# The overflow branch ahead of the last down products, and the last half summed in PSUM by quarters

## The chip, the cores and the metric

One core of one Trainium2 chip runs the program. The time is microseconds (us) of device time for one execution; the kernel before was timed three times, and one further execution was profiled. Every number stored or multiplied is 32-bit float.

## The reference, cut to what matters

A sequence of 256 tokens of 1024 features passes two mixing layers, and then two transformer layers that each end in a mixture of experts. What the change touches is the end of each of those two:

```
y   = hierarchical_moe(h, ...)      # 32 experts: (silu(x @ w_gate[e]) * (x @ w_up[e])) @ w_down[e],
                                    # for the tokens that chose e, each row times its gate,
                                    # summed back over the tokens
x   = layer_norm(ALPHA * x + (1 + g2) * y, ln_g[i, 1], ln_b[i, 1])
```

`w_gate` and `w_up` are 1024 x 512 per expert, `w_down` 512 x 1024: 6 MB an expert, 192 MB a layer, all streamed from HBM.

## The kernel before, in words

The block is written as one instruction list per engine (TensorE, VectorE, ScalarE, GpSimd, SyncE), with semaphores between them. A helper class `Engine` counts what an engine has waited for (`past`) and signalled (`n`). A PSUM bank is taken with `begin(b, name)` (TensorE waits until its last content is drained), signalled with `filled(name)`, and given back by its reader with `drained(name)`.

Experts run in `NQ` = 8 quads of four (`experts(i)`, layer `i` = 0 or 1), with up to `CAP` = 32 tokens of each expert in fixed places. Of a quad `q` TensorE does: the gate and up products of its experts `j` = 0..3 (L920, matmuls of 128 columns, four column groups of 32 at once), a transpose of each hidden tile (`hidden(j)`, L449), a transpose of the gates (`gsT`), the down products of the four experts side by side on the partitions (banks 5 and 6 hold columns 0..511 and 512..1023), and `combine(n)` (L983), which multiplies half `n` with the transposed gates `GST` and so adds it back to the tokens of both token tiles `t`. VectorE multiplies each down half by the gate row `G2` into `YS` (L1062), then adds each combined bank to the running sum `ACC`, which is the array `X` (L1062).

The last quad differs. Its down weights come as three rows of four (`("row", f)`, 2 MB each) and two ends (`("end", n)`, 1 MB each), so that little work is left when the last piece lands. TensorE spreads the two rows of the closing layer norm over the partitions (`norm_row`, L888, banks 1 and 4), does the rows (`down_rows`, L965), the second norm row, the end of half 0 (`down_end`, L973), `combine(0)`, the end of half 1, and `combine(1)`. VectorE follows: multiply, two adds, two `bn_stats` (L1440) for each half, then `last_norm`: two aggregations (L1447), with GpSimd's reciprocal root in parallel, and two passes of `scalar_tensor_tensor` over each token tile's 1024 columns (L1070).

If any expert has over 32 tokens, a slow path `overflow(i)` handles the rest. Whether it runs is read at run time from `cnt`, set early in the layer. TensorE asks after its last `combine` (L1053 and L1054), VectorE after the last quad's hidden tiles (L1822 and L1823), ScalarE and SyncE after their work of the layer. With the inputs here the slow path isn't taken, so each engine jumps over the whole of `overflow`, which is unrolled over 32 experts.

SyncE issues all weight loads, in an order and into slots that a planner fixes beforehand (`plan`); after the last load of layer 0 it asks the same question and then goes on with the loads of the next layer's attention. In layer 0 TensorE's next work after the question is `grouped()`: two gate rows of the attention (L493), which need nothing of the expert stage but free banks, then transposes of `X` (L449).

Of the kernel before, what the change touches and what calls it, by code (L numbers as in the profile page):

```python
# [14 lines left out]
NT = 2  # L15
# [24 lines left out]
NE = 32  # L40
# [88 lines left out]
def program(nc, A, out):  # L129
    with ExitStack() as ctx:  # L130
# [240 lines left out]
        def rows_of_four(i, f):  # L371
            return piece(("dn", i, NQ - 1, "row", f), 4, 1024)
# [61 lines left out]
        def _(eng):  # L434
            pe = Engine(eng, sem("pe"))

            def begin(b, *name):
                if n_results[b]:
                    pe.wait_ge(sem(f"drained{b}"), n_results[b])
                n_results[b] += 1  # L440
                RESULT[name] = b, n_results[b]
                return banks[b]
# [447 lines left out]
            def experts(i):  # L890
# [12 lines left out]
                for q in range(NQ):  # L903
# [39 lines left out]
                    def down(n):  # L943
# [10 lines left out]
                                DONE[name] = filled("dn", i, q, n)  # L954
                        end(ins, "dn", i, q, n)

                    def down_rows():
                        o = [begin(5 + n, "dn", i, q, n) for n in range(2)]
                        for j in range(4):
                            pe.wait_ge(*drained("aT", i, q, j))  # L960
                        for f in range(3):
                            pe.wait_ge(*loaded("dn", i, q, "row", f))
                            for n in range(2):
                                for j in range(4):
                                    ins = eng.matmul(o[n][32 * j:32 * j + 32, :], AT[u][:, j, 32 * f:32 * f + 32],  # L965
                                                     rows_of_four(i, f)[:, j, 512 * n:512 * n + 512], start=f == 0, stop=False)
                            DONE["dn", i, q, "row", f] = pe.step(ins)
                        return o

                    def down_end(o, n):  # L970
                        pe.wait_ge(*loaded("dn", i, q, "end", n))
                        for j in range(4):
                            ins = eng.matmul(o[n][32 * j:32 * j + 32, :], AT[u][:, j, 96:128], ends_of_four(i, n)[:, j, :],  # L973
                                             start=False, stop=True)
                        end(ins, "dn", i, q, n)
                        DONE["dn", i, q, "end", n] = filled("dn", i, q, n)

                    def combine(n):
                        for t in range(NT):
# [3 lines left out]
                            end(eng.matmul(o[:, :], GST[u][:, 128 * t:128 * t + 128], YS[:, 512 * n:512 * n + 512],  # L983
                                           start=True, stop=True), "cb", i, q, n, t)

                    if q == NQ - 1:
                        norm_row(2 * i + 1, 0, LN_OUT[0])
                        o = down_rows()
                        norm_row(2 * i + 1, 1, LN_OUT[1])
                        down_end(o, 0)  # L990
                        combine(0)
                        down_end(o, 1)
                    else:
                        down(0)
                        down(1)
                        combine(0)
                    combine(1)


            def overflow(i):  # L1000
# [45 lines left out]
            for i in range(DEPTH):  # L1046
                if i:
                    grouped()
                else:
                    neighbourhood()  # L1050
                router(i)
                experts(i)
                pe.wait_ge(sem("cnt"), i + 1)  # L1053
                with eng.If(eng.value_load(cnt[0:1, NE:NE + 1]) > CAP):  # L1054
                    overflow(i)

        @block.vector
        def _(eng):
# [662 lines left out]
            def experts(i, chosen):  # L1721
# [17 lines left out]
                for q in range(NQ):  # L1739
# [72 lines left out]
                        combine(1)  # L1812
                        continue

                    def end():
                        for n in range(2):
                            down(n)
                            combine(n)


                    v.wait_ge(sem("cnt"), i + 1)
                    kept = v.n, dict(v.past), v.last  # L1822
                    with eng.If(eng.value_load(cnt[0:1, NE:NE + 1]) > CAP):  # L1823
                        end()
                        overflow(i)
                    v.n, v.past, v.last = kept
                    with eng.Else():
                        end()

            def overflow(i):  # L1830
                o_pe, o_v, o_s = sem(f"o_pe{i}"), sem(f"o_v{i}"), sem(f"o_s{i}")
# [34 lines left out]
                eng.wait_ge(o_pe, O_PE_END)  # L1866


            def last_norm(i):
                for t in range(NT):  # L1870
                    deviation(t)
                for n in range(2):
                    for h in range(2):
                        v.wait_ge(*drained("row", 2 * i + 1, n, h))
                for t in range(NT):
                    v.step(stt(X[:, t, :], X[:, t, :], bn_a[:, t, 0:1], LN_OUT[0], ALU.subtract, ALU.mult))
                v.chain()
                for t in range(NT):
                    v.wait_ge(sem("lrs"), n_dev[0] - 1 + t)
                    ins = stt(X[:, t, :], X[:, t, :], st2[:, t:t + 1], LN_OUT[1], ALU.mult, ALU.add)  # L1880
                    if i + 1 < DEPTH:
                        v.tell(ins, sem("xn"), 3 + t)
                    else:
                        v.tell(ins, sem("xl"), t + 1)
# [3 lines left out]
            for i in range(DEPTH):  # L1888
                if i:
                    grouped()  # L1890
                else:
                    neighbourhood()
                experts(i, router(i))
                last_norm(i)

        @block.scalar
        def _(eng):
# [701 lines left out]
```

## Time and profile before

| | |
|---|---|
| median of 3 runs | 1532.74 us (1531.36 to 1538.42) |
| the profiled execution, its own time | 1536.27 us |
| its span, first to last instruction | 1534.5 us |
| mean granted TensorE clock | 0.951 |
| TensorE busy | 1376.1 us, 90% |
| VectorE busy | 547.8 us, 36% |
| DMA queue of the weights | 519.40 MB |

The span is what the trace covers. A page of the profile names the chain of work that ended last; a timeline gives each merged group of instructions with its start, its length, and in brackets how long its engine had been idle before it and what ended that. PE is TensorE, PEld its weight loads, DVE VectorE, ACT ScalarE, POOL GpSimd, SP SyncE. A 32-bit matmul of the code appears as two MATMUL records.

### The profile page before, as it was taken

What the parts mean: (1) busy time and instruction counts of PE and PEld (TensorE: products, weight loads), DVE (VectorE), ACT (ScalarE), POOL (GpSimd) and SP (SyncE); (2) the same over time, 40 slices, a digit from 0 to 9 for tenths busy, and PEclk for the clock granted to TensorE, in tenths of its full rate; (3) what the DMA queues carried; (4) which work ended last, traced back from release to release, by engine and by line L of the source; (5) the groups of instructions that cost most, each with busy time, mean ns of one, the idle gap of its engine ahead of it and who ended that gap; (6) DMA issues with size and microseconds to landing.
All of it is one profiled execution on the core that took longest, in us unless ns stands there. A gap on an engine that the chain in (4) does not pass through costs nothing.

```text
span 1534.5 us, 28540 instructions
## 1 busy us (share of the span) xinstructions
PE 1376.1 (90%) x12866; PEld 874.1 (57%) x12866; DVE 547.8 (36%) x1251; ACT 218.1 (14%) x578; POOL 85.4 (6%) x91
## 2 busy tenths in 40 slices
PE   7999999999999998879879788878999798798796
PEld 4886488578886555436435443467665363354451
DVE  3596659665843221111111105583211111111113
ACT  3230123022332000000000001442100000000000
POOL 3100111000003000000000001100200000000000
PEclk9999999999999999889889999989999898898997
DMA  9657945778869999999999997237999999999994
GB/s 345 225 195 261 333 171 202 285 267 306 311 270 353 421 427 426 428 426 425 428 426 426 427 399 278 106 121 316 423 410 426 426 426 428 427 426 426 428 420 178
DMA packets 94552, 531.23 MB, mean 346 GB/s; under 512 B 5184, under 2 KB 7424, under 8 KB 70608
## 3 DMA queue, kind: packets, MB, share of 16 engines
q1 hardware_dynamic: 91264, 519.40, 83.8%
q0 software_dynamic: 3152, 9.86, 1.9%
q8 instruction: 105, 1.72, 0.4%
q14 instruction: 31, 0.25, 0.0%
HBM read 528.19 MB, written 1.05 MB: 345 GB/s over the span
## 4 chain that ended last, share of the span: by engine, by line
PE 61%; DMA 29%; DVE 7%; ACT 1%; issue 1%; DVEq 0%; SPq 0%; ACTq 0%
PE bk L453 26%; PE bk L920 16%; DMA AR<-in_moe_w_down 14%; DMA ring<-in_moe_w_down 14%; PE bk L952 8%; PE bk L983 4%; DVE mpart L1070 3%; PE bk L449 2%; PE bk L672 2%; ACT AR L1901 1%; PE bk L687 1%; DVE AR L1062 1%; PE bk L643 1%; DMA ring<-in_w_in 1%; DVE sm L1073 1%
## 5 line engine op out<-in xcount | busy, mean ns | idle before, releaser
L920 PE MATMUL bk<-ring,AR 128*32 128x128 f32 x4480 | 267.5, 409 | 3.1 <-DMA ring<-in_moe_w_up 3.1
L920 PE MATMUL bk<-AR 128*32 128x128 f32 x3712 | 223.0, 409 | 4.8 <-DMA AR<-in_moe_w_up 4.0
L1062 DVE TENSOR_TENSOR AR<-bk,AR 128x128 f32<-128x128 f32 (+2 forms) x106 | 41.3, 390 | 516.9 <-ACT AR L1901 450.4
L920 PEld LDWEIGHTS bk<-ring,AR 128*32 128x32 f32 x4480 | 175.4, 127 | 85.6 <-DMA ring<-in_moe_w_up 5.6
L453 PE MATMUL bk<-ring,AR 128*128 128x256 f32 (+2 forms) x736 | 214.3, 449 | 5.7 <-ACT AR L1901 2.6
L1901 ACT ACTIVATE AR<-bk 128x512 f32<-128x512 f32 (+4 forms) x182 | 75.3, 436 | 931.9 <-PE bk L920 755.9
L920 PEld LDWEIGHTS bk<-AR 128*32 128x32 f32 x3712 | 144.8, 127 | 75.3 <-DMA AR<-in_moe_w_up 6.2
L453 PEld LDWEIGHTS bk<-ring,AR 128*128 128x128 f32 x736 | 141.3, 195 | 71.4 <-issue 54.4
L952 PE MATMUL bk<-ring,AR 128*32 128x512 f32 x544 | 137.5, 704 | 43.1 <-DMA ring<-in_moe_w_down 43.1
L453 PE MATMUL bk<-AR,ring 128*128 128x256 f32 (+1 forms) x832 | 170.6, 364 | 1.6 <-DVE diag L1062 1.6
L453 PEld LDWEIGHTS bk<-AR,ring 128*128 128x128 f32 x832 | 147.4, 190 | 21.4 <-issue 3.5
L952 PE MATMUL bk<-AR 128*32 128x512 f32 x352 | 130.8, 714 | 27.4 <-DMA AR<-in_moe_w_down 27.4
L1070 DVE SCALAR_TENSOR_TENSOR mpart<-ring,ccol,mpart 128x512 f32<-128x512 f32 x168 | 130.3, 776 | 6.0
L1062 DVE TENSOR_TENSOR AR<-bk,mpart 128x512 f32<-128x512 f32 x32 | 22.1, 691 | 218.8 <-PE bk L952 191.4
L952 PEld LDWEIGHTS bk<-ring,AR 128*32 128x32 f32 x544 | 31.0, 126 | 103.3 <-DMA ring<-in_moe_w_down 57.8
L449 PE MATMUL bk<-cst,AR 128*128 128x128 f32 (+1 forms) x356 | 63.9, 292 | 22.6 <-DVE AR L1746 12.0
L449 PEld LDWEIGHTS bk<-cst,AR 128*128 128x128 f32 (+1 forms) x356 | 41.3, 142 | 57.3 <-issue 26.2
L453 PE MATMUL bk<-AR 128*128 128x128 f32 (+1 forms) x536 | 71.2, 292 | 0.6 <-DVE AR L1062 0.5
L952 PEld LDWEIGHTS bk<-AR 128*32 128x32 f32 x352 | 28.4, 127 | 72.5 <-DMA AR<-in_moe_w_down 38.5
L453 PEld LDWEIGHTS bk<-AR 128*128 128x128 f32 x536 | 65.9, 199 | 4.7 <-issue 2.6
L983 PE MATMUL bk<-AR 128*128 128x512 f32 x128 | 61.1, 619 | 5.0 <-DVE AR L1062 5.0
L643 PE MATMUL bk<-ring,AR 128*128 128x512 f32 x128 | 55.5, 594 | 0.0
(161 smaller groups left out, 892.0 us busy)
## 6 DMA issues: line engine op xcount, KB each, us to landing
ring<-in_moe_w_gate SPq DMA_DIRECT2D x36, 2048.0 KB, 30.0
ring<-in_moe_w_up SPq DMA_DIRECT2D x34, 2048.0 KB, 26.8
AR<-in_moe_w_up SPq DMA_DIRECT2D x30, 2048.0 KB, 29.6
ring<-in_moe_w_down SPq DMA_DIRECT2D x30, 2048.0 KB, 34.2
AR<-in_moe_w_gate SPq DMA_DIRECT2D x28, 2048.0 KB, 27.3
AR<-in_moe_w_down SPq DMA_DIRECT2D x26, 2048.0 KB, 34.0
ring<-in_ada_w SPq DMA_DIRECT2D x24, 2048.0 KB, 10.7
ring<-in_w_in SPq DMA_DIRECT2D x12, 2048.0 KB, 14.4
```

The costliest lines, as they stand in the source:

```text
L449: return eng.transpose(o, a, ident[0:k, 0:k])
L453: ins = eng.matmul(o, l, r, start=i == 0, stop=i == len(pairs) - 1)
L643: ins = eng.matmul(o[:, :], BIG[:, x, OUTS[m] + 128 * t:OUTS[m] + 128 * t + 128], w[:, 2 * m + x, :], start=k + x == 0, stop=k + x == 4)
L672: ins = eng.matmul(o[b][:, a * nk:(a + 1) * nk], g["q"][h][:, t * 128:(t + 1) * 128], g["k"][h][:, 0:nk], start=True, stop=True)
L687: ins = eng.matmul(o[64 * b:64 * b + 64, 128 * x:128 * x + 128], g["v"][2 * x + b][kt], ET[j % 2][:, (2 * b + x) * nkt + kt, :], start=kt ...
L920: ins = eng.matmul(o[32 * f:32 * f + 32, 128 * m:128 * m + 128], XG[u][:, c, 32 * j:32 * j + 32], w[:, c, f::4], start=c == 0, stop=c == N ...
L952: ins = eng.matmul(o[32 * j:32 * j + 32, :], AT[u][:, j, 32 * f:32 * f + 32], w, start=f == 0, stop=f == 3)
L983: end(eng.matmul(o[:, :], GST[u][:, 128 * t:128 * t + 128], YS[:, 512 * n:512 * n + 512], start=True, stop=True), "cb", i, q, n, t)
L1062: return eng.tensor_tensor(o, a, b, op)
L1070: return eng.scalar_tensor_tensor(out=o, in0=a, scalar=s, in1=b, op0=op0, op1=op1)
L1073: return eng.tensor_reduce(o, a, AX, op)
L1901: return eng.activation(o, a, f, **kw)
```

## The change

Both ends of the last quad are rewritten.

On TensorE the question whether there is overflow is asked before the last quad's down products, and everything after it stands in both arms (`ending()`; `overflow(i)` follows in one of them). Inside `ending()`, two products with the identity first put the running sum of half 1 (`ACC[:, t, 512:1024]`) into banks 2 and 3 and leave them open. Half 1 of the down products is split into two quarters of 256 columns, in banks 6 and 0; `combine(1)` becomes `end_sums`, which adds each quarter's product with the gates onto the open banks, quarter by quarter.

On VectorE the multiply of half 1 comes in two quarters, and the adds of half 1 are gone: `bn_stats` reads the banks, and `last_norm`, now in both arms, reads half 1 of its first pass from the banks too. In the overflow arm the banks are copied to `ACC` first.

```diff
--- before.py
+++ after.py
@@ -954,26 +954,48 @@
                                 DONE[name] = filled("dn", i, q, n)
                         end(ins, "dn", i, q, n)
 
+                    halves = ((0, (("dn", i, q, 0), 5, 0, 512)), (1, (("quarter", i), 6, 512, 256)), (1, (("dn", i, q, 1), 0, 768, 256)))
+
                     def down_rows():
-                        o = [begin(5 + n, "dn", i, q, n) for n in range(2)]
+                        o = [begin(b, *name)[:, 0:c] for n, (name, b, c0, c) in halves]
                         for j in range(4):
                             pe.wait_ge(*drained("aT", i, q, j))
                         for f in range(3):
                             pe.wait_ge(*loaded("dn", i, q, "row", f))
-                            for n in range(2):
+                            for k, (n, (name, b, c0, c)) in enumerate(halves):
                                 for j in range(4):
-                                    ins = eng.matmul(o[n][32 * j:32 * j + 32, :], AT[u][:, j, 32 * f:32 * f + 32],
-                                                     rows_of_four(i, f)[:, j, 512 * n:512 * n + 512], start=f == 0, stop=False)
+                                    ins = eng.matmul(o[k][32 * j:32 * j + 32, :], AT[u][:, j, 32 * f:32 * f + 32],
+                                                     rows_of_four(i, f)[:, j, c0:c0 + c], start=f == 0, stop=False)
                             DONE["dn", i, q, "row", f] = pe.step(ins)
                         return o
 
                     def down_end(o, n):
                         pe.wait_ge(*loaded("dn", i, q, "end", n))
-                        for j in range(4):
-                            ins = eng.matmul(o[n][32 * j:32 * j + 32, :], AT[u][:, j, 96:128], ends_of_four(i, n)[:, j, :],
-                                             start=False, stop=True)
-                        end(ins, "dn", i, q, n)
+                        for k, (m, (name, b, c0, c)) in enumerate(halves):
+                            if m == n:
+                                for j in range(4):
+                                    ins = eng.matmul(o[k][32 * j:32 * j + 32, :], AT[u][:, j, 96:128],
+                                                     ends_of_four(i, n)[:, j, c0 - 512 * n:c0 - 512 * n + c], start=False, stop=True)
+                                end(ins, *name)
                         DONE["dn", i, q, "end", n] = filled("dn", i, q, n)
+
+                    def begin_sums():
+                        o = []
+                        for t in range(NT):
+                            o.append(begin((2, 3)[t], "cb", i, q, 1, t))
+                            pe.wait_ge(*drained("cb", i, q - 1, 1, t))
+                            eng.matmul(o[t][:, :], ident, ACC[:, t, 512:1024], start=True, stop=False)
+                        return o
+
+                    def end_sums(o):
+                        pe.wait_ge(*drained("gsT", i, q))
+                        for c0 in (0, 256):
+                            pe.wait_ge(*(drained("dn", i, q, 1) if c0 else drained("quarter", i)))
+                            for t in range(NT):
+                                ins = eng.matmul(o[t][:, c0:c0 + 256], GST[u][:, 128 * t:128 * t + 128],
+                                                 YS[:, 512 + c0:768 + c0], start=False, stop=c0 > 0)
+                                if c0:
+                                    end(ins, "cb", i, q, 1, t)
 
                     def combine(n):
                         for t in range(NT):
@@ -983,18 +1005,31 @@
                             end(eng.matmul(o[:, :], GST[u][:, 128 * t:128 * t + 128], YS[:, 512 * n:512 * n + 512],
                                            start=True, stop=True), "cb", i, q, n, t)
 
-                    if q == NQ - 1:
+                    if q < NQ - 1:
+                        down(0)
+                        down(1)
+                        combine(0)
+                        combine(1)
+                        continue
+
+                    def ending():
+                        sums = begin_sums()
                         norm_row(2 * i + 1, 0, LN_OUT[0])
                         o = down_rows()
                         norm_row(2 * i + 1, 1, LN_OUT[1])
                         down_end(o, 0)
                         combine(0)
                         down_end(o, 1)
-                    else:
-                        down(0)
-                        down(1)
-                        combine(0)
-                    combine(1)
+                        end_sums(sums)
+
+                    pe.wait_ge(sem("cnt"), i + 1)
+                    kept = pe.n, dict(pe.past), pe.last, list(n_results)
+                    with eng.If(eng.value_load(cnt[0:1, NE:NE + 1]) > CAP):
+                        ending()
+                        overflow(i)
+                    pe.n, pe.past, pe.last, n_results[:] = kept
+                    with eng.Else():
+                        ending()
 
 
             def overflow(i):
@@ -1050,9 +1085,6 @@
                     neighbourhood()
                 router(i)
                 experts(i)
-                pe.wait_ge(sem("cnt"), i + 1)
-                with eng.If(eng.value_load(cnt[0:1, NE:NE + 1]) > CAP):
-                    overflow(i)
 
         @block.vector
         def _(eng):
@@ -1812,20 +1844,35 @@
                         combine(1)
                         continue
 
-                    def end():
-                        for n in range(2):
-                            down(n)
-                            combine(n)
+                    def end(stored):
+                        down(0)
+                        combine(0)
+                        v.wait_ge(*filled("cb", i, q - 1, 1, 1))
+                        for k, name in enumerate((("quarter", i), ("dn", i, q, 1))):
+                            v.wait_ge(*filled(*name))
+                            free(tt(YS[:, 512 + 256 * k:768 + 256 * k], bank(*name)[:, 0:256], G2[1][:, 256 * k:256 * k + 256],
+                                    ALU.mult), *name)
+                        for t in range(NT):
+                            o = bank("cb", i, q, 1, t)[:, :]
+                            v.wait_ge(*filled("cb", i, q, 1, t))
+                            if stored:
+                                free(eng.tensor_copy(ACC[:, t, 512:1024], o), "cb", i, q, 1, t)
+                                v.chain()
+                                v.step(stats(t, 1, ACC))
+                            else:
+                                v.step(eng.bn_stats(bn_s[:, t, 1, :], o))
 
 
                     v.wait_ge(sem("cnt"), i + 1)
-                    kept = v.n, dict(v.past), v.last
+                    kept = v.n, dict(v.past), v.last, n_dev[0]
                     with eng.If(eng.value_load(cnt[0:1, NE:NE + 1]) > CAP):
-                        end()
+                        end(True)
                         overflow(i)
-                    v.n, v.past, v.last = kept
+                        last_norm(i, True)
+                    v.n, v.past, v.last, n_dev[0] = kept
                     with eng.Else():
-                        end()
+                        end(False)
+                        last_norm(i, False)
 
             def overflow(i):
                 o_pe, o_v, o_s = sem(f"o_pe{i}"), sem(f"o_v{i}"), sem(f"o_s{i}")
@@ -1866,14 +1913,19 @@
                 eng.wait_ge(o_pe, O_PE_END)
 
 
-            def last_norm(i):
+            def last_norm(i, stored):
                 for t in range(NT):
                     deviation(t)
                 for n in range(2):
                     for h in range(2):
                         v.wait_ge(*drained("row", 2 * i + 1, n, h))
                 for t in range(NT):
-                    v.step(stt(X[:, t, :], X[:, t, :], bn_a[:, t, 0:1], LN_OUT[0], ALU.subtract, ALU.mult))
+                    if stored:
+                        v.step(stt(X[:, t, :], X[:, t, :], bn_a[:, t, 0:1], LN_OUT[0], ALU.subtract, ALU.mult))
+                        continue
+                    v.step(stt(X[:, t, 0:512], X[:, t, 0:512], bn_a[:, t, 0:1], LN_OUT[0][:, 0:512], ALU.subtract, ALU.mult))
+                    free(stt(X[:, t, 512:1024], bank("cb", i, NQ - 1, 1, t)[:, :], bn_a[:, t, 0:1], LN_OUT[0][:, 512:1024],
+                             ALU.subtract, ALU.mult), "cb", i, NQ - 1, 1, t)
                 v.chain()
                 for t in range(NT):
                     v.wait_ge(sem("lrs"), n_dev[0] - 1 + t)
@@ -1891,7 +1943,6 @@
                 else:
                     neighbourhood()
                 experts(i, router(i))
-                last_norm(i)
 
         @block.scalar
         def _(eng):
```

## Rows read from the trace of the kernel before

**Rows 1.** the page: GB/s in 40 slices; last chain by engine
```profile
GB/s 345 225 195 261 333 171 202 285 267 306 311 270 353 421 427 426 428 426 425 428 426 426 427 399 278 106 121 316 423 410 426 426 426 428 427 426 426 428 420 178
...
PE 61%; DMA 29%; DVE 7%; ACT 1%; issue 1%; DVEq 0%; SPq 0%; ACTq 0%
```

**Rows 2.** the chain that ended last: start, us, what
```profile
926.99 4.92 issue
```

**Rows 3.** timeline, PE, layer 0: start, us, what, count [idle before]
```profile
905.35 0.33 PE L449 MATMUL bk<-cst,AR 128*128 128x128 f32 x1 [0.52 <-DVE AR L1778]
...
905.61 1.98 PE L888 MATMUL bk<-AR,ones 1*128 1x512 f32 x4
...
907.52 3.62 PE L965 MATMUL bk<-ring,AR 128*32 128x512 f32 x16
...
914.75 1.92 PE L965 MATMUL bk<-AR 128*32 128x512 f32 x16 [1.89 <-DMA AR<-in_moe_w_down]
...
920.48 1.96 PE L983 MATMUL bk<-AR 128*128 128x512 f32 x4 [0.91 <-DVE AR L1062]
...
922.37 1.06 PE L973 MATMUL bk<-ring,AR 128*32 128x512 f32 x8
...
925.01 1.99 PE L983 MATMUL bk<-AR 128*128 128x512 f32 x4 [1.57 <-DVE AR L1062]
...
931.91 2.08 PE L493 MATMUL bk<-diag,ones 64*128 64x512 f32 x4 [4.92 <-issue]
...
933.92 3.68 PE L449 MATMUL bk<-cst,X 128*128 128x128 f32 x16
```

**Rows 4.** timeline, SyncE at the same end: the issue of DMAs
```profile
900.62 0.51 SPq L2495 DMA_DIRECT2D ring<-in_moe_w_down  x1
...
906.91 15.00 SPq L2404 DMA_DIRECT2D ring<-in_gqa_w_qkv  x3
```

**Rows 5.** timeline, layer 1's last quad, PE
```profile
1500.43 0.33 PE L449 MATMUL bk<-cst,AR 128*128 128x128 f32 x1 [0.52 <-DVE AR L1778]
...
1509.96 1.92 PE L965 MATMUL bk<-AR 128*32 128x512 f32 x16 [0.38 <-DMA AR<-in_moe_w_down]
...
1511.81 1.98 PE L888 MATMUL bk<-AR,ones 1*128 1x512 f32 x4
...
1515.69 3.38 PE L983 MATMUL bk<-AR 128*128 128x512 f32 x4 [0.90 <-DVE AR L1062]
```

**Rows 6.** timeline, PE: 64 products of 128 columns in four groups
```profile
887.14 7.57 PE L920 MATMUL bk<-AR 128*32 128x128 f32 x128
```

**Rows 7.** windows: length, busy of five engines, granted clock, DMA, GB/s
```profile
907.00:908.00 1.00, 1.00 (x6) 0.19 (x8) 0.00 (x0) 0.74 (x2) 0.00 (x0) 0.79 1.03 395
...
911.00:912.00 1.00, 1.00 (x16) 0.35 (x12) 0.00 (x0) 0.00 (x0) 0.00 (x0) 1.00 0.85 332
...
931.00:932.00 1.00, 0.09 (x2) 0.12 (x2) 1.00 (x1) 0.00 (x0) 0.40 (x1) 0.74 1.05 391
...
1501.00:1502.00 1.00, 1.00 (x3) 0.40 (x2) 0.09 (x1) 0.00 (x0) 0.00 (x0) 0.75 1.02 403
...
1508.00:1509.00 1.00, 1.00 (x16) 0.21 (x8) 0.00 (x0) 0.00 (x0) 0.00 (x0) 0.84 0.58 229
```

**Rows 8.** timeline, layer 0's end, DVE
```profile
923.08 1.28 DVE L1440 BATCH_NORM_STATS2 st<-X 128x6 f32<-128x512 f32 x2
...
924.28 0.68 DVE L1062 TENSOR_TENSOR AR<-bk,mpart 128x512 f32<-128x512 f32 x1
...
927.63 1.28 DVE L1440 BATCH_NORM_STATS2 st<-X 128x6 f32<-128x512 f32 x2
...
929.71 5.00 DVE L1070 SCALAR_TENSOR_TENSOR X<-X,st,AR 128x1024 f32<-128x1024 f32 x4
```

**Rows 9.** groups by form, DVE: what xcount | busy us, mean ns | idle
```profile
L1062 DVE TENSOR_TENSOR AR<-bk,AR 128x256 f32<-128x256 f32 x24 | 10.2, 423 | 39.1 <-PE bk L453 38.2 <-PE bk L687 0.7
...
L1070 DVE SCALAR_TENSOR_TENSOR X<-X,bk 128x512 f32<-128x512 f32 x8 | 5.5, 688 | 1.7 <-PE bk L983 1.7
```

## The prediction

> **What bounds the kernel now.** I read the page first: bytes a second and the last chain by engine. While experts stream, the core moves about 426 GB/s slice after slice, and the chain goes through TensorE and DMA with little else [rows 1]. So time lost or won at the end of a layer, where the next layer or the output waits for it, is not paid back by a faster stream: the loads of the second layer's experts wait for slots that its attention frees. Second, the chain in order of time: right after layer 0's last combine it has a piece called issue, 4.92 us in which TensorE waits for nothing that the profile knows [rows 2]. Third, the timelines of both layer ends on TensorE, SyncE and VectorE. The reader is to see three things there. The last hidden transpose ends at 905.68 (layer 0) and 1500.76 (layer 1). The third row of down weights is then waited for, but barely: 1.89 us in layer 0, 0.38 us in layer 1, so the last matmuls on it end at 916.67 and 1511.88 [rows 3, 5]. Behind that TensorE and VectorE alternate until the norm.
>
> **The moved branch.** The 4.92 us lie exactly where the overflow question stands now: between the last record of `combine` (ends 926.99) and the gate rows of the next attention (931.91). Those gate rows need a diagonal that VectorE wrote long before and banks that were drained before 926.99. I take the time as the price of load, compare and jump on TensorE. A second row bounds it: SyncE asks the same question after its last issue (ends 901.13) and issues the next load at 906.91, into a slot whose last reader, the up products of expert 29, was long done; that is 5.8 us [rows 4]. SyncE asks it while the stream is full, at nearly the place to which TensorE's question moves. So TensorE's costs 4.9 us from the end of the last transpose, or 5.8 us from its start (the sequencer can run ahead of the array): it restarts at 910.6 to 911.15, I take 910.9; in layer 1 at 1505.7 to 1506.2, I take 1506.0. Queued behind it on TensorE is everything that is left of the layer, and VectorE and ScalarE wait for that; SyncE and GpSimd are not moved past.
>
> The Trainium skill speaks on both sides here. "Runtime: NRT & Kernel Launch", section Instruction fetch mechanics, says that a taken jump to code outside the small window of fetched instructions has to wait for a DMA fetch; the jump here passes the unrolled slow path, and the rows agree in sign. "Advanced Engine Details and Errata", section Control Flow Timing, gives about 108 ns for a compare and branch; at that price the branch would vanish from the sum (second rival).
>
> **What TensorE does before the third row is done.** In the changed kernel, from its restart:
> - two identity products of 512 columns, four records like `combine(0)`'s, whose successor starts 1.89 us later (920.48 to 922.37) [rows 3]: 1.9 us, new;
> - the first norm row: 905.61 to 907.52, 1.9 us, as before;
> - three rows of down weights. Sixteen records of 512 columns take 1.85 us at full clock (1509.96 to 1511.81) [rows 5]. Now eight of 512 and sixteen of 256: the first eight cost 0.93 us; for the others the floor is the issue, 7.57 us / 128 = 0.059 us a record [rows 6], 0.94 us. That is 1.87 us, I take 1.9 with some slack: 5.7 us for three.
> That is 9.5 us at full clock. The weights are there by then: the third row landed at 914.7 and 1509.9.
>
> The clock is the unsure term. In layer 0 it fell to half (1.2 GHz) within 907 to 908 and was back at 911; in layer 1 it fell within 1501 to 1502 and was back only in 1508 to 1509; after the 4.9 us of idling at the branch it fell again, at 931 to 932 [rows 7]. A mean of 0.79 in a window between full and half says that it fell at 907.6, and 0.75 and 0.84 that it was low from 1501.5 to 1508.3. Both stretches (3.4 and 6.8 us) lay in the shadow of the third row's landing. Now TensorE idles first and then has work it can't hide, so half of the half-clock time is lost: 1.7 to 3.4 us if the whole stretch falls on work, 0.9 us if part of it falls into the idling. I take 2.2 us in each layer. Sum: layer 0 910.9 + 9.5 + 2.2 = 922.6, 5.9 us later than 916.67; layer 1 1506.0 + 9.5 + 2.2 = 1517.7, 5.8 us later than 1511.88. The cover that was used up is 1.9 and 0.4 us of waiting and the slow clock's shadow; all else is on the path.
>
> **What the new end saves.** Half 1's multiply can't start before VectorE has done half 0's statistics (923.08 to 924.36), as now at 924.28 [rows 8]. A multiply of 256 columns takes 0.42 us [rows 9], pitch about 0.34: both quarters are ready at 924.70 and 925.04. TensorE adds the first quarter for two tiles (half of 1.89: 0.9 us, from 924.75), then the second, tile 0 ready about 926.15, tile 1 about 926.6. `bn_stats` on the banks then runs to about 927.5. Now it ends at 928.91 [rows 8]. A saving of 1.4 us. Reading statistics from PSUM has no row; on VectorE a 512-wide pass from a bank takes 688 ns [rows 9], and `bn_stats` from `X` takes 1.28 us for two, so I bound the difference by 0.1 us either way. The closing pass of two 1024-wide instructions (pitch 1.25 us) [rows 8] becomes four of 512 (pitch about 0.6 to 0.69, by the 688 ns row): from 0 to 0.3 us more, I take 0.1. Net 1.3 us a layer. The half-1 end itself (sixteen records of 256 for eight of 512) costs 0 to 0.1 us, hidden by the statistics that the multiply waits for.
>
> Layer 0 also gets back part of the old branch: the gate rows at 931.91 to 933.99 held back the transposes of `X`, ready at about 933.5 (929.71 [rows 8] and three passes of 1.25 us) and started at 933.92 [rows 3], and the ScalarE copies behind them. Taken with the earlier `X` I count 1.8 us there in place of 1.3, with 0 to 0.3 us more possible. In layer 1 the branch lay beside the norm and gives nothing back. Layer 1's `combine(0)` ran at half clock, 3.38 us, where layer 0's took 1.96 [rows 3, 5]; in the change it may or may not, so half of 1.4, 0.7 us, is counted as a gain.
>
> **Sum.** Layer 0: +5.9 - 1.8 = +4.1. Layer 1: +5.8 - 1.3 - 0.7 = +3.8. Together +7.9 us. The profiled execution's own time is 1536.27 us (span 1534.5 plus 1.8 around it), which gives 1544.2; it lies 3.5 us above the median but inside the runs. The terms are differences, so I put them on the median, 1532.74, and round up: 1541 us. Lowest terms (restart at 910.6 and 1505.7, clock loss 0.9, tail 1.4 and 1.9, clock gain 1.4): +3.8, 1536.5. Highest (911.15 and 1506.2, clock loss 3.4, tail 0.9 and 1.4, no clock gain, 0.1 more in the rows): +12.5, 1545.2.
>
> **Rivals.**
> *More half clock.* For: with TensorE later, pieces like `combine(0)` with 0.9 us gaps on both sides may fall into half clock in both layers, 1.4 us each, as layer 1's did [rows 5]; the low stretch can last 6.8 us [rows 7]. Against: the same gaps in layer 0 passed at full clock. Time: the sum's upper half plus 1.4 to 2.8, 1545 to 1549, about 1546.
>
> *The branch is cheap where it goes, so not slower.* The mechanism: the jump's price at 926.99 is something of that place (a fetch into the next layer's code), and TensorE restarts at once behind the last transpose. Then only the identity products delay it. Layer 0's third row could begin at 912.86 (914.75 - 1.89), now 914.85: 0.1 us late. Layer 1's at 1509.58 plus 1.9 to 3.4 us (full or half clock), 1511.5 to 1513.0 for 1509.96: about 2.4 us late. With the gains of 1.8 and 2.0 this is +0.1 - 1.8 + 2.4 - 2.0 = -1.3: 1531.5, between 1529.5 and 1533. It decides from a branch of under 1 us. For: VectorE asks at the same point and the trace shows no price for it, though its wait for the down products would hide one. Against: SyncE's 5.8 us. The 108 ns that the Trainium skill gives would lead here too.
>
> *The new end fails to shorten.* If reading PSUM or the open banks made VectorE wait, the tail would save 0 in place of 1.3 us a layer: +10.5, 1543. Against: the 512-wide pass with a bank as operand takes no more than its share of the 1024-wide one from `X` (688 ns of 1.25 us, with a fixed part in both) [rows 8, 9].
>
> **How the numbers follow.** Forecast 0.65, more half clock 0.15, cheap branch 0.13, no shorter end 0.07. The measurement tells 0.5%, 7.7 us: 1525.1 and 1540.4. The forecast's own range, 1536 to 1546, is split by 1540.4 nearly in the middle; with 0.15 and 0.07 all above it, slower by over 0.5% gets 0.52, no difference 0.44, faster 0.04 (even the cheap branch gives only 1 to 3 us). Range 1532 to 1547: it leaves out the lower half of the cheap branch and the end of more half clock.
>
> **What would show it.** Right: in the changed trace TensorE idles some 5 us with "issue" between the last hidden transpose and the first identity product in both layers; the third down row starts without a wait for DMA, about 5 to 6 us later than now; the gate rows L493 follow the last sums with under 1 us of idling; statistics end about 1.4 us sooner after the second end's products. Wrong: idling of under 1 us in front of the identity products (second rival), a third row that still waits for its DMA, or a granted clock that stays full.

## The result, and the profile after

The changed kernel took 1554.41 us (median of 4, 1552.67 to 1558.16) against 1535.58 us of the kernel before on the same chip (median of 4, 1531.36 to 1538.48): ratio 1.0125, 95% interval 1.0102 to 1.0148, or +18.8 us at the medians. The direction was forecast, the size was not: +7.9 us was said, and 1547 was the end of the range.

The page of the changed kernel, its span and the last chain by engine:

```profile
span 1551.5 us, 28698 instructions
...
PE 65%; DMA 24%; DVE 8%; issue 2%; ACT 1%; DVEq 0%; SPq 0%; ACTq 0%
```

Against [rows 1] the chain has more TensorE and less DMA, but that tells little: a run below that is no slower than the kernel before (e8) has 63% and 26%, with layer 0's third row still waiting 1.92 us for its DMA. The timelines decide.

The timeline of TensorE at layer 0's last quad, changed kernel, beside [rows 3]:

```profile
900.86 0.33 PE L449 MATMUL bk<-cst,AR 128*128 128x128 f32 x1 [0.52 <-DVE AR L1810]
...
907.56 3.78 PE L987 MATMUL bk<-X,cst 128*128 128x512 f32 x4 [6.37 <-issue]
...
911.27 3.78 PE L888 MATMUL bk<-AR,ones 1*128 1x512 f32 x4
...
918.39 3.89 PE L967 MATMUL bk<-AR 128*32 128x512 f32 x48
...
922.21 1.98 PE L888 MATMUL bk<-AR,ones 1*128 1x512 f32 x4
...
926.09 3.48 PE L1005 MATMUL bk<-AR 128*128 128x512 f32 x4 [0.90 <-DVE AR L1094]
...
929.50 1.07 PE L977 MATMUL bk<-ring,AR 128*32 128x256 f32 x16
...
933.79 1.13 PE L493 MATMUL bk<-diag,ones 64*128 64x512 f32 x4
...
939.68 3.48 PE L449 MATMUL bk<-cst,X 128*128 128x128 f32 x16 [4.75 <-DVE X L1102]
```

Identity products, norm row and down rows now stand in a line without a wait for DMA. (A group x48 on L967 holds two rows of down weights, 24 records each.) I count from the start of the last transpose, since single executions reach it some us apart (905.35 before, 900.86 here), to the last record on the third row: 11.3 us before (905.35 to 916.67), 21.4 us now (900.86 to 922.28). Layer 1, beside [rows 5]:

```profile
1508.38 0.33 PE L449 MATMUL bk<-cst,AR 128*128 128x128 f32 x1 [0.52 <-DVE AR L1810]
...
1514.88 3.78 PE L987 MATMUL bk<-X,cst 128*128 128x512 f32 x4 [6.17 <-issue]
...
1525.72 4.01 PE L967 MATMUL bk<-AR 128*32 128x512 f32 x48
...
1529.66 1.98 PE L888 MATMUL bk<-AR,ones 1*128 1x512 f32 x4
...
1533.54 3.54 PE L1005 MATMUL bk<-AR 128*128 128x512 f32 x4 [0.90 <-DVE AR L1094]
```

It was 11.45 us (1500.43 to 1511.88) and is 21.4 us (1508.38 to 1529.73). So each layer's third row is done 10 us later after the transpose, where 5.8 and 5.9 were forecast. The windows show why; the granted clock is the first number behind the five engines:

```profile
901.00:902.00 1.00, 0.19 (x1) 0.00 (x0) 0.29 (x1) 0.00 (x0) 0.00 (x0) 0.93 0.99 393
...
918.00:919.00 1.00, 1.00 (x12) 0.36 (x8) 0.00 (x0) 0.00 (x0) 0.00 (x0) 0.54 1.06 399
...
1509.00:1510.00 1.00, 0.00 (x0) 0.00 (x0) 0.04 (x1) 0.00 (x0) 0.00 (x0) 0.72 1.01 395
...
1526.00:1527.00 1.00, 1.00 (x12) 0.15 (x8) 0.00 (x0) 0.00 (x0) 0.00 (x0) 0.75 0.00 0
```

A mean between 0.5 and 1 tells how much of that microsecond was at half clock (1.2 GHz). The clock falls 0.7 us into the idling, at 901.9 and 1509.4, is at 0.50 in every window between, and comes back only at 918.9 and 1526.5: 17.1 us each, of which 11.4 and 11.6 us are work (907.56 to 918.9, 1514.88 to 1526.5).

VectorE at layer 0's end, beside [rows 8]:

```profile
930.21 1.28 DVE L1472 BATCH_NORM_STATS2 st<-X 128x6 f32<-128x512 f32 x2
...
933.47 1.29 DVE L1863 BATCH_NORM_STATS2 st<-bk 128x6 f32<-128x512 f32 x2 [1.32 <-PE bk L995]
...
935.57 0.75 DVE L1102 SCALAR_TENSOR_TENSOR X<-X,st,AR 128x512 f32<-128x512 f32 x1
...
938.34 2.48 DVE L1102 SCALAR_TENSOR_TENSOR X<-X,st,AR 128x1024 f32<-128x1024 f32 x2
```

From the start of the last end products to the last statistics: 922.37 to 928.91 before, 6.5 us; 929.50 to 934.76 now, 5.3 us; layer 1 has the same two numbers. The new end saves its 1.3 us.

### The profile page after: what moved, and what is told of

Its sections match the earlier page's. It is cut to its first block, busy times and chain, and to the rows that moved or that the text cites. A ratio compares the mean times of both kernels' runs of the same rounds, so it can differ in the third digit from the quotient of the medians.

```text
span 1551.5 us, 28698 instructions
## 1 busy us (share of the span) xinstructions
PE 1385.7 (89%) x12946; PEld 883.4 (57%) x12946; DVE 545.7 (35%) x1253; ACT 217.8 (14%) x578; POOL 84.4 (5%) x91
## 4 chain that ended last, share of the span: by engine, by line
PE 65%; DMA 24%; DVE 8%; issue 2%; ACT 1%; DVEq 0%; SPq 0%; ACTq 0%
PE bk L453 26%; PE bk L920 19%; DMA ring<-in_moe_w_down 14%; DMA AR<-in_moe_w_down 9%; PE bk L952 8%; PE bk L1005 4%; DVE mpart L1102 3%; PE bk L449 2%; PE bk L672 1%; ACT AR L1952 1%; DVE AR L1094 1%; PE bk L687 1%; PE bk L967 1%; PE bk L643 1%; PE bk L888 1%
## 5 line engine op out<-in xcount | busy, mean ns | idle before, releaser
L453 PE MATMUL bk<-ring,AR 128*128 128x256 f32 (+2 forms) x736 | 210.4, 443 | 5.5 <-ACT AR L1952 2.7
L453 PEld LDWEIGHTS bk<-AR,ring 128*128 128x128 f32 x832 | 147.4, 190 | 21.4 <-issue 3.5
L1094 DVE TENSOR_TENSOR AR<-bk,mpart 128x512 f32<-128x512 f32 (+1 forms) x34 | 22.2, 659 | 239.8 <-PE bk L952 192.4
## 6 DMA issues: line engine op xcount, KB each, us to landing
ring<-in_ada_w SPq DMA_DIRECT2D x24, 2048.0 KB, 10.9
ring<-in_w_in SPq DMA_DIRECT2D x12, 2048.0 KB, 14.7
```

Of the source, the lines that this page charges most:

```text
L453: ins = eng.matmul(o, l, r, start=i == 0, stop=i == len(pairs) - 1)
L1094: return eng.tensor_tensor(o, a, b, op)
```

## The experiments

All ratios are to the kernel before on the same chip, whose medians were 1537.08 (e1 to e4), 1537.54 (e6 to e9) and 1535.59 us (e5, e10, e12). A signed time is the ratio less 1, times this median; the difference of the two medians can lie up to 3 us off it. The diffs are abridged. "Transpose to third row" is the interval of the section above: 11.3 and 11.45 us before, 21.4 and 21.4 in the changed kernel. Theory A: the question idles TensorE where it has no slack, and the idling drops the clock over the work behind it. Theory B: the identity products are what costs.

**e1, only the question moves.**

```diff
 # kernel before, TensorE, last quad
+def ending():                      # the old end, unchanged
+    norm_row(0); down_rows; norm_row(1); down_end(0); combine(0); down_end(1); combine(1)
+pe.wait_ge(sem("cnt"), i + 1)
+with eng.If(count > CAP):
+    ending()
+    overflow(i)
+with eng.Else():
+    ending()
```

> Only the question moves: TensorE asks before the last quad's down products, with the old end in both arms; no identity products, no quarters. Theory A (the question idles TensorE for about 6.4 us and the clock is then at half over the work behind it): the third down row is done 6 to 7 us later after the last transpose than in the kernel before, in each layer, and combine(0) may fall into half clock too (1.5 us); layer 0 gets 1 to 2 us back from the old place. Sum +11 to +16 us. Theory B (the identity products in front of the rows are what costs, the question is largely hidden by the wait for the weights): +0 to +5 us.

1551.41 us, ratio 1.0102 (1.0084 to 1.0119), +15.7 us. TensorE, layer 0:

```profile
901.39 0.33 PE L449 MATMUL bk<-cst,AR 128*128 128x128 f32 x1 [0.52 <-DVE AR L1787]
...
908.07 3.78 PE L888 MATMUL bk<-AR,ones 1*128 1x512 f32 x4 [6.35 <-issue]
...
911.77 3.64 PE L965 MATMUL bk<-ring,AR 128*32 128x512 f32 x16
...
915.19 3.96 PE L965 MATMUL bk<-AR 128*32 128x512 f32 x32
```

The idle is 6.35 us, norm row and first down row run at half clock (3.7 and 3.4 us to the next group), and the third row is done 17.8 us (layer 1: 17.6 us) after the transpose: +6.3 a layer. The clock was at half for 13.7 us (902.2 to 915.9), the last 7.8 of them with work. `combine(0)` took 3.53 us in layer 0, 1.6 us more than in [rows 3]. Theory A holds; the question alone makes about four fifths of the loss (0.0102 of 0.0125).

**e2, only the new end.**

```diff
 # changed kernel, TensorE
-with eng.If(...): ending(); overflow(i)
-with eng.Else(): ending()
+ending()                           # question behind it, as before
```

> Only the new end: identity products, quarters, statistics and norm from the banks; TensorE asks after the end, as before. Theory A: no idle in front, so the identity products cost 1.9 us, in layer 0 under the wait for the third row, in layer 1 1.5 to 3.4 us on the path; the tails save 1.3 us each. Sum -1 to +2 us against the kernel before. Theory B: +10 us or more.

1534.92 us, ratio 0.9984 (0.9968 to 1.0000), -2.5 us: a little under the expected -1 to +2, and with an interval that ends at 1. Theory B falls. TensorE in layer 1, and then the old question's place in layer 0:

```profile
1501.58 0.33 PE L449 MATMUL bk<-cst,AR 128*128 128x128 f32 x1 [0.52 <-DVE AR L1806]
...
1501.75 1.88 PE L987 MATMUL bk<-X,cst 128*128 128x512 f32 x4
...
1510.23 1.93 PE L967 MATMUL bk<-AR 128*32 128x512 f32 x24 [1.11 <-DMA AR<-in_moe_w_down]
```

```profile
932.07 2.08 PE L493 MATMUL bk<-diag,ones 64*128 64x512 f32 x4 [5.28 <-issue]
```

The identity products start 0.17 us behind the transpose and run at full clock (1.88 us), and the third row still waits 1.11 us for its DMA: they cost nothing on the path. The question is back behind the end, 5.28 us. `combine(0)` is at half clock in both layers here too (3.53 and 3.65 us), with no question in front: so full or half clock there varies between runs with the question behind the end, and its 1.5 us can't be booked to the question alone.

**e3, the jump made short.**

```diff
 with eng.If(count > CAP):
     ending()
-    overflow(i)
```

> The changed kernel without the slow path in TensorE's overflow arm (it is left out there, so the arm is a few hundred instructions); load, compare and both arms stay. If the price of the question is the jump past the unrolled slow path (code has to be fetched): the idle in front of the identity products falls from 6.4 us to 1 to 2.5 us, and the time to about +5 to +9 us over the kernel before. If it is the load of the count and the compare: it stays near 6.4 us and +18 us.

1538.46 us, ratio 1.0019 (0.9995 to 1.0044), not told apart from the kernel before and under the +5 to +9 us that I expected. TensorE, layer 0:

```profile
901.98 0.33 PE L449 MATMUL bk<-cst,AR 128*128 128x128 f32 x1 [0.52 <-DVE AR L1809]
...
903.45 1.98 PE L987 MATMUL bk<-X,cst 128*128 128x512 f32 x4 [1.14 <-issue]
...
911.38 1.93 PE L967 MATMUL bk<-AR 128*32 128x512 f32 x24 [0.46 <-DMA AR<-in_moe_w_down]
```

The idle is 1.14 us here and 0.54 us in layer 1. From the start of the transpose to the first identity product it is 1.5 and 0.9 us, where the changed kernel has 6.7 and 6.5. So load, compare, two arms and a jump over a few hundred instructions are cheap; over 5 us come with the jump past the unrolled slow path. The clock stays full, the third row waits for its DMA again, and it is done 11.3 and 11.4 us after the transpose, as in the kernel before: nothing is left of the 10 us a layer.

The Trainium skill states in "Runtime: NRT & Kernel Launch", section Instruction fetch mechanics, that a taken jump out of the window of fetched instructions stalls until its target is fetched by DMA. These rows agree with it; they show the dependence on the distance, not the fetch itself. The Trainium skill's 108 ns for a compare and branch, in "Advanced Engine Details and Errata", section Control Flow Timing, are not what either question cost here (0.54 us of idle at the least).

**e4, the array kept busy over the question.**

```diff
+busy(8, 5)       # 8 identity products of 512 columns into bank 5, used by nobody
 pe.wait_ge(sem("cnt"), i + 1)
```

> The changed kernel with eight more identity products of 512 columns (16 records, 6.9 us at full clock) issued just before the question, into a free bank; their results are used by nobody. If TensorE's sequencer runs ahead of its array, the array works while the question is answered, the clock stays full, and the third row is done 4 to 5 us sooner in each layer than in the changed kernel: about +9 us over the kernel before. If the question waits for the array to drain: the idle of 6.4 us follows the products, and the time is +25 us or more (theory A holds on the idle but the clock can't be saved so).

1542.93 us, ratio 1.0040 (1.0022 to 1.0057), +6 us. TensorE, layer 0:

```profile
902.06 0.33 PE L449 MATMUL bk<-cst,AR 128*128 128x128 f32 x1 [0.52 <-DVE AR L1811]
...
902.23 7.03 PE L869 MATMUL bk<-cst 128*128 128x512 f32 x16
...
909.10 1.88 PE L987 MATMUL bk<-X,cst 128*128 128x512 f32 x4
...
914.56 3.63 PE L967 MATMUL bk<-AR 128*32 128x512 f32 x48
```

Sixteen records fill 902.23 to 909.26 and the real work follows with no gap: the sequencer answers the question while the array works. All is at full clock, 16.1 us from transpose to third row in both layers, 5.3 us less than in the changed kernel, though the real work begins 7.0 us behind the transpose and not 6.7. Up to the third row this run keeps the delay and takes away only the slow clock. From the first identity product to the third row it is 9.1 us here and 14.7 us in the changed kernel (907.56 to 922.28): 5.6 us a layer is the slow clock's price. The total is below the +9 us expected: twice 5.3 us at the third rows, and 1.5 us more because `combine(0)` took 1.95 us in layer 0, at full clock.

**e5, without the identity products.**

```diff
-eng.matmul(o[t][:, :], ident, ACC[:, t, 512:1024], start=True, stop=False)
 ...
-    start=False, stop=c0 > 0)
+    start=c0 == 0, stop=c0 > 0)
```

> The changed kernel without the two identity products: the running sum of half 1 is left out of the result, all else stays. If they cost what they take at half clock and nothing else: third row 3.7 us sooner after the last transpose in each layer, about -7 us against the changed kernel, +10 to +11 us against the kernel before. If the clock comes back by the clock time and not by the work done, the stretch at half clock shifts onto the down rows, and they save only about 2 us a layer: +14 us. The rival in which the identity products are the main cost: +2 us or less.

1549.11 us, ratio 1.0081 (1.0054 to 1.0109), +12.4 us; the result lacks the running sum of half 1. Transpose to third row 17.9 and 18.1 us, close to e1, and the clock at half for 13.7 us as there. In the changed kernel, behind the idling, the products cost about 3.4 us a layer, a little less than the 3.7 us that they take at half clock; in e2 they cost nothing.

**e6 and e8, the question where TensorE waits anyway.**

```diff
 # TensorE, experts(i): the body of the loop over quads becomes quad(q) -> front, back
+for q in range(6): front(q); back(q)
+front(6)
+with eng.If(count > CAP): back(6); front(7); back(7); overflow(i)
+with eng.Else():          back(6); front(7); back(7)
```

> The changed kernel with the question one quad earlier on TensorE, in front of the seventh quad's down products, everything behind it in both arms. There TensorE waits some 7 us for down weights in any case. Theory A (the price is idling and slow clock where TensorE has no slack): the 6.4 us lie inside that wait, the last quad runs as in e2, and layer 0 has no question behind its end: -2 to -4 us against the kernel before, 13 us or more faster than the changed kernel. Rival (the two arms or the jump cost wherever they stand): +6 us or more.

> The kernel before with its question moved in front of the seventh quad's down products, old end unchanged. Theory A: hidden by the wait for weights, and layer 0's end is rid of its 4.9 us idle, of which 0.5 to 1 us was on the path: -0.5 to -1.5 us against the kernel before. Rival as for e6: +6 us.

e6 (new end): 1534.09 us, ratio 0.9993 (0.9973 to 1.0012). e8 (old end): 1538.50 us, ratio 1.0014 (0.9999 to 1.0029). e6 in the seventh quad of layer 0, and its last quad:

```profile
842.25 3.74 PE L453 MATMUL bk<-AR 128*128 128x128 f32 x32
...
850.55 1.03 PE L953 MATMUL bk<-AR 128*32 128x512 f32 x1 [4.57 <-issue]
```

```profile
902.69 0.33 PE L449 MATMUL bk<-cst,AR 128*128 128x128 f32 x1 [0.52 <-DVE AR L1823]
...
911.86 1.93 PE L968 MATMUL bk<-AR 128*32 128x512 f32 x24 [1.63 <-DMA AR<-in_moe_w_down]
...
925.36 1.13 PE L493 MATMUL bk<-diag,ones 64*128 64x512 f32 x4
```

The same question idles TensorE for 4.57 us in front of the down products (4.58 in layer 1), and a DMA wait of 2.98 us follows; the kernel before waits for down weights there twice, 3.65 and 3.85 us. Both make 7.5 us. In the last quad nothing is late: the third row waits 1.63 us for its DMA. The rival (a cost wherever it stands) falls: 6 us were not there. The small gain that I expected of ridding layer 0 of its old question does not show, and e6's -2 to -4 us is not reached either; neither run differs clearly from the kernel before.

**e7 and e9, the identity products earlier.**

```diff
 for j in range(4):
+    if q == NQ - 1 and j == 2:
+        sums.extend(begin_sums())            # banks 0 and 6 in place of 2 and 3
 ...
-halves: banks 5, 6, 0
+halves: banks 5, 2, 3
```

> As e6, and the identity products are issued in the middle of the last quad's gate and up products (before its third expert) into banks 0 and 6, the quarters going to banks 2 and 3. If the 1.9 us of identity products were still partly on the path in e2 and e6: 0.5 to 2 us faster than e6. If they were hidden by the wait for the third row: the same as e6 within 0.5 us, or slower, since the last quad's gate and up products have little slack.

> e2 (new end, question behind the end as in the kernel before) with the identity products in the middle of the last quad, as in e7. Against e2: -0.5 to -1.5 us if they were on the path in layer 1, +0 to +1.5 us if the last quad's gate and up products are what they delay.

e7: 1535.35 us, ratio 0.9983 (0.9972 to 0.9994), no clear step from e6 (0.9993). e9: 1533.51 us, ratio 0.9981 (0.9967 to 0.9994), -2.9 us: the lowest ratio of all and, like e7's, an interval free of 1, but no clear step from e2 (0.9984). TensorE of e9, layer 1:

```profile
1499.84 0.33 PE L449 MATMUL bk<-cst,AR 128*128 128x128 f32 x1 [0.52 <-DVE AR L1818]
...
1500.10 3.10 PE L888 MATMUL bk<-AR,ones 1*128 1x512 f32 x4
...
1509.70 1.93 PE L970 MATMUL bk<-AR 128*32 128x512 f32 x24 [0.71 <-DMA AR<-in_moe_w_down]
```

The third row still waits here, 0.71 us: the identity products were hidden already, and putting them earlier frees nothing. Part of the time goes to the clock: with no identity products behind the transpose it fell at 1500.8, and norm row and first down row took 3.0 and 3.4 us, where e2 did them at full clock in 1.9 and 1.7 us.

**e10, the one-row products behind the down rows.**

```diff
+o = down_rows()
 norm_row(2 * i + 1, 0, LN_OUT[0])
-o = down_rows()
 norm_row(2 * i + 1, 1, LN_OUT[1])
```

> The changed kernel with the first norm row (four records with one row of weights) issued behind the three down rows and not in front of them. In the changed trace the granted clock was at half over identity products (3.7 us), norm row (3.7) and two of the three down rows. If the one-row products held the clock down: it is back to full about 3.4 us sooner, and the time falls by 1.5 to 4 us in each layer, +11 to +15 us over the kernel before. If not, the order is indifferent: +18 us, and the clock is at half for 11 us of work again.

1553.61 us, ratio 1.0100 (1.0066 to 1.0134), an interval that reaches past the changed kernel's 1.0125: in all not told apart from it. TensorE and windows, layer 0:

```profile
904.16 0.33 PE L449 MATMUL bk<-cst,AR 128*128 128x128 f32 x1 [0.52 <-DVE AR L1810]
...
910.95 3.78 PE L987 MATMUL bk<-X,cst 128*128 128x512 f32 x4 [6.46 <-issue]
...
917.49 3.62 PE L967 MATMUL bk<-AR 128*32 128x512 f32 x48
```

```profile
916.00:917.00 1.00, 1.00 (x12) 0.36 (x8) 0.00 (x0) 0.00 (x0) 0.00 (x0) 0.56 1.05 395
...
923.00:924.00 1.00, 1.00 (x4) 0.43 (x4) 0.00 (x0) 0.60 (x1) 0.00 (x0) 0.85 0.95 326
...
933.00:934.00 1.00, 1.00 (x12) 0.19 (x4) 1.00 (x3) 0.00 (x0) 0.00 (x0) 0.53 1.02 375
```

The clock came back at 916.9, after 5.9 us of work and not 11.4, and the third row is done 17.0 us after the transpose (16.3 in layer 1) with the norm row still to do. But it fell again at 923.7, over the two norm rows in a row, and was low for another 10.2 us, over `combine(0)` and both ends. The first part of the expectation held, the gain was given back. Whether the one-row products are the reason is not shown: one order was changed, and the clock also fell later in the idling, 2.2 us into it (906.6) against 0.7 us in the changed kernel.

**e12, useful work ahead of the question.**

```diff
+sums = begin_sums()
+norm_row(2 * i + 1, 0, LN_OUT[0])
 def ending():
-    sums = begin_sums()
-    norm_row(2 * i + 1, 0, LN_OUT[0])
```

> The changed kernel with the identity products and the first norm row (3.8 us of work at full clock, which the rest needs anyway) issued ahead of the question. As e4 showed, the sequencer answers the question while its array works: the idle falls from 6.4 to about 2.7 us, the clock stays full or falls for a short stretch. Third row done 13 to 15 us after the last transpose begins, in place of 21.4 (11.3 in the kernel before): +2 to +6 us against the kernel before.

1541.88 us, ratio 1.0041 (1.0020 to 1.0061), +6.3 us. TensorE, layer 0:

```profile
902.36 0.33 PE L449 MATMUL bk<-cst,AR 128*128 128x128 f32 x1 [0.52 <-DVE AR L1811]
...
902.53 1.88 PE L987 MATMUL bk<-X,cst 128*128 128x512 f32 x4
...
909.89 3.64 PE L967 MATMUL bk<-ring,AR 128*32 128x512 f32 x24 [3.57 <-issue]
...
913.31 4.52 PE L967 MATMUL bk<-AR 128*32 128x512 f32 x48
```

3.8 us of needed work hide under the question, and 3.57 us of idle are left. The clock still fell (its windows have it at half from 908.3 to 915.1, 6.8 us): 15.5 and 14.5 us to the third row, where 13 to 15 were expected.

## Why the prediction was wrong, by its steps

**The moved branch: right in kind, too small.** Idle "issue" stands in front of the first identity product in both layers, as forecast. It is 6.7 and 6.5 us from the start of the transpose (907.56 - 900.86, 1514.88 - 1508.38), where I took 5.55: about +1 us a layer. The 4.92 us at the old place [rows 2] and SyncE's 5.8 us [rows 4] were not bounds. e4 shows that the sequencer can be at the question while the array still works, so part of the time at the old place may have lain beside `combine`; that part was not measured, and why SyncE's figure is shorter no run shows.

**Work in front of the third row: right.** 9.5 us at full clock were said; e4 shows 9.1 us (909.10 to 918.19), 0.4 us less, with three rows, the norm row and the identity products.

**The clock: the step that failed.** "I take 2.2 us in each layer", with 3.4 us as the highest. Measured: 11.4 us of work at half clock, 5.7 us lost; e4, with nearly the same delay and a full clock, puts it at 5.6 us. I had taken two stretches in the trace of before (3.4 and 6.8 us, [rows 7]) for the length that a stretch can have, with neither of them behind a long idle, and had let part of it run down during the idle. The windows show it at half through the whole idle and over 11.4 us of work behind it. The length differed from run to run: 17.1 us in the changed kernel, 13.7 in e1 and e5, 10.2 in e10, 6.8 in e12; why it is so long here stays open. The trace of before had a nearer case that I read only at its start: behind the 4.92 us of idle at the old question the clock fell at 931.5 [rows 7] and came back at 938.3,

```profile
938.00:939.00 1.00, 0.81 (x2) 0.54 (x3) 1.00 (x5) 1.00 (x5) 0.00 (x0) 0.85 1.04 381
```

so 6.4 us at half lay behind the restart at 931.91 there, all but 0.6 us of them work: some 2.9 us of loss, worked out as for the changed kernel. The term was 3.4 us a layer too small, 6.8 of the 10.9 us that were missing. Of the rest some 2 us are the branch, and some 3 us lie behind the third rows, where -1.8 and -2.0 were forecast and +0.15 and -0.85 came.

**The gains: the ends right, `combine(0)` not.** 1.4 us a layer was said of the statistics and 1.3 us measured. The closing pass took 0.3 us more, the upper end of its term: four instructions of 512 fill 935.57 to 938.34, 2.77 us, for two of 1024 at 1.25. Counted besides was 0.7 us for a layer 1 `combine(0)` at full clock; instead it was at half in both layers (3.48 and 3.54 us beside 1.96 and 3.38 in [rows 3, 5]), as the first rival said, 1.5 us in layer 0. It was so in e2 as well, so the forecast counted on a clock that changes from run to run. From the end of the third row to the transposes of `X`, layer 0 took 17.25 us before and 17.4 now.

**The sum with measured terms.** Layer 0: +10.1 to the third row and +0.15 behind it. Layer 1: +9.9, and from the third row to the end of the span 21.8 us (1529.73 to 1551.5) after 22.6 (1511.88 to 1534.5), -0.85. That is +19.3 us, against +18.8 of the medians. So close an agreement is partly luck: it leaves out that this execution reached layer 0's transpose 4.5 us sooner than the one of before and took 2.2 us more from the transposes of `X` to layer 1's last quad (568.7 us after 566.5; the other runs have 566.3 to 571.4), which makes +17.0 us between the two spans.

**The rivals.** The cheap branch is refuted by the changed kernel's own trace and by e1: 6.2 to 6.4 us of idle. "More half clock" named the right quantity but began from the same short stretch, so 1549 was its end. A new end that fails to shorten is refuted by VectorE's rows (6.5 us before, 5.3 us now); e2's total, -2.5 us with an interval up to 0, fits.

## What to carry to other kernels

A run-time question in front of an unrolled slow path costs its engine about 6.5 us here; it is free only where the engine waits for something else by more than that (e6). Work issued ahead of it hides it as far as that work is needed anyway (3.8 us in e12), and kept the clock full when it filled the whole time (e4). On TensorE count the idle twice: the idle itself, and half of the work behind it until the clock is back, which was nearly as much again (5.6 us). A clock stretch seen in the trace of before belongs to the load of before, and gave no upper bound for a new idle in front of other work (17.1 us after 6.8).

## What the runs showed of the hardware

- The price of the same question on TensorE by what the jump passes: 6.2 to 6.4 us of idle over the slow path's code, 0.5 to 1.1 us over a few hundred instructions (e3).
- TensorE's sequencer got past a load, a compare and a jump while its array worked off 16 records, 7 us (e4), with no gap behind them.
- The granted clock stayed at half for 17.1 us around 6.4 us of idle, with TensorE busy in the last 11.4 of them.
- `bn_stats` on a PSUM bank took 1.29 us for two of 512 columns, on SBUF 1.28 us.
